# RWKV's core beside the gate tiles: four steps of front per chunk, and both pairs of heads at the same rows

## The reference, cut to what matters

```
S_t = S_{t-1} diag(w_t) + (S_{t-1} a_t) b_t^T + v_t k_t^T ;   y_t = S_t r_t
a = -kk,  b = kk * a_gate,  kk = k*k_k / max(sqrt(sum(kk*kk)), 1e-12)
```

## Time and profile before

| | us |
|---|---|
| median of 3 runs | 2084.71 (2082.78 to 2092.68) |
| the profiled execution | 2090.74 |
| its span | 2089.0 |
| TensorE busy in it | 2033.5 (97%) |
| VectorE, ScalarE, GpSimd busy | 983.1, 775.4, 278.3 |
| mean granted clock of TensorE | 0.985 of full speed |
| the chain that ended last, TensorE's share | 88% |

### The profile page before, as it was taken

The page is one execution under the profiler, slowest core; times in us unless marked ns, Lnnn a source line. Parts: engine busy times, 40 slices in busy tenths (PEclk is TensorE's granted clock), DMA queues, the critical chain, the costliest instruction groups (busy, mean ns, idle before and its releaser), DMA issues.

```text
span 2089.0 us, 27641 instructions
## 1 busy us (share of the span) xinstructions
PE 2033.5 (97%) x11572; PEld 1631.0 (78%) x11572; DVE 983.1 (47%) x1549; ACT 775.4 (37%) x1233; POOL 278.3 (13%) x279
## 2 busy tenths in 40 slices
PE   8989999999999999999999999999899999999997
PEld 6767677777788778888778888888688888888886
DVE  6655555444553233336754544445643432333365
ACT  5573222123444332234533333334322343322345
POOL 1001221210221000012200000001310120100123
PEclk9999999899999999999999999999999999999999
DMA  5111111111633332222421212222232233223221
GB/s 187 57 65 61 47 47 47 41 47 52 222 101 104 101 106 95 97 100 92 161 71 61 71 61 81 84 79 70 81 101 95 98 117 115 101 91 101 92 95 56
DMA packets 59972, 185.47 MB, mean 89 GB/s; under 512 B 6551, under 2 KB 11799, under 8 KB 59720
## 3 DMA queue, kind: packets, MB, share of 16 engines
q1 hardware_dynamic: 59848, 183.71, 26.0%
HBM read 173.46 MB, written 10.22 MB: 88 GB/s over the span
## 4 chain that ended last, share of the span: by engine, by line
PE 88%; DVE 4%; ACT 4%; issue 2%; POOL 1%; DMA 1%; SPq 0%; DVEq 0%; POOLq 0%; ACTq 0%
PE P L561 25%; PE P L563 24%; PE P L562 24%; DVE AREN L1705 1%; PE P L849 1%; PE P L885 1%; POOL AREN L2425 1%; PE P L939 1%; DVE AREN L1708 1%; PE P L878 1%; PE P L937 1%; PE P L834 1%; ACT WHI L1133 1%; PE P L1062 1%; PE P L1028 1%
## 5 line engine op out<-in xcount | busy, mean ns | idle before, releaser
L561 PE MATMUL P<-HH,WHI 128*128 128x512 f32 x1528 | 623.0, 408 | 10.7 <-DVE HL L1725 3.8
L563 PE MATMUL P<-HH,WLO 128*128 128x512 f32 x1528 | 602.2, 394 | 0.0
L562 PE MATMUL P<-HL,WHI 128*128 128x512 f32 x1528 | 601.7, 394 | 0.0
L1133 ACT ACTIVATE WHI<-RAW 128x1024 fp32r<-128x1024 f32 x302 | 317.9, 1053 | 438.3 <-PE P L563 437.5
L1712 DVE TENSOR_TENSOR WLO<-RAW,WHI 128x1024 fp32r<-128x1024 f32 x302 | 374.8, 1242 | 144.6 <-ACT WHI L1133 143.1
L561 PEld LDWEIGHTS P<-HH,WHI 128*128 128x128 f32 x1528 | 289.9, 190 | 89.0 <-issue 15.9
L561 PE MATMUL P<-ARR,WHI 128*128 128x512 f32 (+1 forms) x920 | 353.8, 385 | 0.0
L563 PE MATMUL P<-ARR,WLO 128*128 128x512 f32 (+1 forms) x920 | 352.9, 384 | 0.0
L562 PE MATMUL P<-ARR,WHI 128*128 128x512 f32 (+1 forms) x920 | 352.8, 383 | 0.0
L563 PEld LDWEIGHTS P<-HH,WLO 128*128 128x128 f32 x1528 | 290.3, 190 | 63.1
L562 PEld LDWEIGHTS P<-HL,WHI 128*128 128x128 f32 x1528 | 290.7, 190 | 55.5 <-issue 0.2
(11 more groups left out here) (304 smaller groups left out, 1555.6 us busy)
## 6 DMA issues: line engine op xcount, KB each, us to landing
RAW<-in_w_in_dram SPq DMA_DIRECT2D x117, 512.0 KB, 3.2
RAW<-in_w_ff_dram SPq DMA_DIRECT2D x64, 512.0 KB, 3.2
RAW<-in_w_ml_dram SPq DMA_DIRECT2D x64, 512.0 KB, 3.2
RAW<-in_w_out_dram SPq DMA_DIRECT2D x16, 512.0 KB, 3.2
RAW<-in_w_pg_dram SPq DMA_DIRECT2D x16, 512.0 KB, 3.2
AREN<-in_xT_dram SPq DMA_DIRECT2D x16, 256.0 KB, 5.7
s_gates<-AREN SPq DMA_DIRECT2D x16, 256.0 KB, 2.0
RAW<-in_w_ab_dram SPq DMA_DIRECT2D x8, 512.0 KB, 3.4
```

Of the source, the lines that this page charges most:

```text
L561: e.matmul(out, hi, H[0][:, s], start=first, stop=False)
L562: e.matmul(out, hi, H[1][:, s], start=False, stop=False)
L563: return e.matmul(out, lo, H[0][:, s], start=False, stop=last)
L1133: e.activation(WHI[n % NSPL][:, :], RAW[n % NRAW][:, :], ACT.Copy).then_inc(*D.act.sig("whi", n))
```

## The change

```
-    seq = [["f"], ["f"], ["f"]]
+    seq = [["f"], ["f"], ["f"], ["f"]]
     for what, q, lev in core_steps():
-        seq.append(["c"] + (["f"] if q < 3 and (what in "WN" or (what, lev) == ("la", 3)) else []))
+        seq.append(["c"] + (["f"] if q < 3 and (what in "WN" or (what, lev) in (("la", 3), ("lb", 4))) else []))
     n = len(seq)
-    late = [A_GA + 4 + i * 121 // n for i in range(n)]
-    early = list(range(A_RW + 68, A_GA + 2, 2))
-    rest = n - len(early)
     for i, group in enumerate(seq):
-        put_at = early[i] if i < len(early) else late[(i - len(early)) * (n - 2) // rest]
-        put_steps(at, put_at, group, 0)
-    for i, group in enumerate(seq):
-        put_steps(at, late[i], group, 1)
+        for jj in range(2):
+            put_steps(at, A_GA + 4 + i * 121 // n, group, jj)
@@ tensor_program, front(jj)
                 for q in range(4):
+                    yield
                     b = 6 + jj
                     w.wait_ge(F.act.at("sq", q), free.get(b))
                     (the sum of squares, L781)
@@ pool_program, front(jj)
-                    yield
-                    yield
+                    for _ in range(3):
+                        yield
```

## The result

| | before | after |
|---|---|---|
| median of 6 runs each, us | 2084.86 (2082.78 to 2092.68) | 2075.92 (2072.13 to 2077.07) |
| ratio to before, 95% interval | | 0.9943 (0.9926 to 0.9961) |
| profiled execution, its span | 2090.74, 2089.0 | 2077.07, 2075.3 |

The change makes the kernel faster, by 0.6% by the ratio and 9 us by the medians. Ten more runs of the changed kernel in another batch gave 2076.03 (2074.5 to 2079.39) and 0.9949 (0.9931 to 0.9966). I had forecast 2088, "same". The time lies in the range that I gave, but on the other side of the time before, and where the third rival (the clock behaves as now, 2074) had put it.

What follows compares the result with a forecast made beforehand. It took TensorE as the bound, 88% of the chain and hardly idle in the region. Terms -11.2 - 4.4 + 7.3 + 13 = +4.7, taken as +3.5 us, made 2088 us from 2084.7; range 2073 to 2109.

Steps and rivals of the forecast that it cites:

- the third rival: Clock behaves as now: one fall of 8 us per double O, or falls only behind gaps; about 2074 us, chance 0.15.
- The front's wait: TensorE's wait ahead of L781 goes, 11.2 us over 8 fronts, since a step in between gives cover: -11.2 us.
- The new waits: Both pairs at once: +5.5 us at chunk 0, +3 in chunks 1 to 3, -1.2 at M; +7.3 us.
- Fewer switches: 22 fewer dense rows interrupted by small steps, at 0.2 us each: -4.4 us.
- The clock: Double O's each bring a fall, three of 17.9 us and one of 9, 63 us at half clock: +13 us.
- the main term: The clock's falls; named wrong if intervals at half clock add up to under 45 or over 80 us.
- the signs that I had named: Gate's stage near 314 us, its clock near 0.90, four half-clock intervals of 17 to 18 us but for the last.
- my mark of 2: Forecast wrong altogether if merge or later stages change by over 2 us.
- The rival with the clock staying down: Clock low for most of each chunk from chunk 0's G on: 2109 us, chance 0.25.
- VectorE as the bound: In the gate's stage both pairs' VectorE operations come together, waits +20 us instead of +7.3: 2100 us, chance 0.10.

Runs made afterwards that it cites:

- each half of the change alone: Against the kernel before: only the four steps of front, ratio 0.9921; or only both pairs at the same rows, front in three steps, ratio 0.9999.
- chunk 0's front early: Changed kernel with chunk 0's four lone front steps moved ahead into RWKV's own rows, 180 to 208: 2076.03 us, ratio 0.9936.
- the kernel with four steps of front alone: Four steps of front, but pair 0 keeps its early rows and the rest as before: 2070.06 us, ratio 0.9921 against the kernel before.
- pair 1 a group behind: Changed kernel with pair 1 one group behind pair 0, so no two O steps stand together: 2076.84 us, ratio 0.9950 to the kernel before.
- first row with O in halves: Four steps of front with the rows of before, and each O step cut into two steps of 16 matmuls: 2068.75 us, ratio 0.9917.
- the two kernels with quarters: Changed kernel with each O in four parts, 2064.17 us; the same plus chunk 0's front early and front's second step at lb level 3, 2054.23 us.

## Why the prediction was wrong

**The front's wait** (forecast -11.2): right. L777 waits twice, 1.6 us, both in chunk 0, where the forecast had them.

**The new waits** (+5.5, +3): right in kind, a little high. Chunk 0 costs 1.6 at L777 and 2.7 at G, 4.3 in all; the later chunks 2.3. The place was off: not la's third level behind VectorE but the fourth of lb behind ScalarE's operations. The larger miss is on the other side of the account: the kernel before had 5.5 us of other waits in the region, and I credited only the 1.2 at M and put the other 4.3 at nothing, without a reason. All went, so waits are -11.4 together and not the -3.9 of my terms. In each half of the change alone the waits other than that for the square come to 3 us, so pair 0's place in RWKV's rows alone doesn't explain them.

**Fewer switches** (-4.4 at 0.2 us for each of 22 rows): right in kind, low in size: -7.4, which is 0.34 us a row if all of it is switches. That is no price for an interruption in general: cutting O in quarters interrupts twelve rows more and costs 1.8 us, 0.15 each, less than the 0.23 that I had read at the edges. What makes up the difference no run here takes apart.

**The clock** (+13): the step that failed, with the waits that I left at nothing. Half of it held. Every double O brought a fall, in both traces of the changed kernel, 4.5 to 6.1 us into it in the first, while a single O brings one only sometimes. But the length did not hold. "The clock came back only behind stretches of two dense rows; G (L834) did not raise it" was read from a place where one pair's O stands alone, and made 17.9 us of each fall and 63 in all. Measured are 10.2, 6.8, 10.2 and 10.2 us, and with chunk 0's 3.4 it is 41 (44.4 in the second trace). By the mark that I had set, under 45, the main term is wrong. The place was no fair sample: of the falls at single O's with two dense rows and a G behind them, those at 376.4 and 444.7 did last through G, but the one at 315.0 was back in it, and I had that row and did not weigh it. This is it, in the kernel before:

```profile
314.60 0.51 PE L561 MATMUL P<-HH,WHI 128*128 128x512 f32 x1
314.94 0.59 PE L562 MATMUL P<-HL,WHI 128*128 128x512 f32 x1
...
317.17 2.25 PE L834 MATMUL P<-AREN 64*128 64x128 f32 x16
319.35 0.50 PE L561 MATMUL P<-HH,WHI 128*128 128x512 f32 x1
```

G takes 2.18 us from start to start, between its 1.64 at full and 3.02 at half clock. The fall also began in the dense row behind O, where I had written that it never fell outside O. And a double O is not the same place. In the earlier trace rows the clock fell 1.2 us ahead of the first dense row; in the changed kernel it fell 5.6 us ahead of it (277.2 against 282.80), and so had been down for longer when G came. That this is the reason isn't shown: with chunk 0's front early one fell 5.2 us ahead of it (414.8 against 420.0) and still outlasted G. With both pairs at the same rows, two dense rows behind the O's had the clock back within 1.8 us of G's start in 10 of 11 places of five traces; with one row it came back 3.7 to 4.8 us into G or, in one case, 8.9 us behind G's start. What each fall's length hangs on beyond that I did not settle. In the two traces of the region the clock costs 16.5 us after against 12.6 before, +3.9 instead of +13; by the clocks of all runs, over the whole kernel, it is about +8.

In sum, in the region's traces, the clock term was 9 us too high, waits 7.5 and switches 3, which is 20 us. The sum for the region was +4.7 and came out at -15. Outside it the kernel got 3 us longer, which I had at nothing. With the clock at +8 and all else as forecast, my terms would still have given no change; the waits and the switches turned it into a gain. The range held the time since it reached to the case where the clock term is nothing. Of the signs that I had named, the clock over the gate's stage is 0.93 (near 0.90 forecast) and the stage 293 us (near 314). The first merge rows (336 to 399) take 2.5 us more than before in the first pair of traces and 1.1 in the second, the first of these over my mark of 2: TensorE's wait for the weights' low part there is 2.5 us instead of 1.8, and a fall of 3.4 us stands right behind it.

The time is that of the third rival, but its mechanism is only half of what happened, and that the time fits is luck. It had the clock cost what it cost before (measured +3.9 in the region, about +8 in all), and waits and switches that were too high by as much made up for that. It had one fall of 8 us at each double O, or falls only behind gaps; there was one at each, of 6.8 to 10.2 us, and without a gap. The Trainium skill ("TensorE: Matmul & The Clock Gate", section "Why this matters for your kernels") ties falls to idle gaps. Here some falls do stand beside gaps: the one at 222.6 stands behind waits of 0.8 and 1.9 us and went when those were taken away, and in the kernel with four steps of front alone one at 256.1 stands at a wait of 2.2 us. But the four large ones begin where TensorE has been busy without a gap, and cutting that run into pieces removed them with the waits left standing (8.2 us against 6.9).

The rival with the clock staying down is refuted: no fall outlasts 10.2 us in the two traces of the changed kernel. VectorE as the bound too: TensorE's waits for it are 0.8 us in the region.

**What stays open.** In one of the eleven places (chunk 0's front early, in the interval that holds 420.0) the clock stayed down through G in spite of two rows ahead. At some single O's a fall comes in one execution and not in the next, and a run of 4.1 us brought one at all four places when a single row and the other pair's O followed. What sets that, and how long a fall lasts, is open.

## What to carry to other kernels

When steps of a serial recurrence ride between dense work, count the unbroken run of small matmuls that a new order makes: two runs of 4 us put together cost clock each time (20 of 20 places), and the same work in pieces of 2 us did not. Give a stage whose operand is made by two other engines a step of its own ahead of its use before joining streams. As long as the clock moves by itself, taking out a wait of 2 to 4 us may not show; settle the clock first and then take the waits. And read the clock of every run, not only of the traced one: it told here what single traces did not.

## What the runs showed of the hardware

- TensorE's clock fell with the engine 100% busy: at each of the 20 places with a run of O's 64-wide 32-bit matmuls of 8.2 us at full clock, in five traces; at 8 of 16 with a run of 4.1 us in the two traces of the kernel before (in it or up to 0.4 us behind it); at none of the 32 with a run of 2.06 us in the two kernels with quarters.
- It stayed at half for 23.9 us with the engine busy for all of them, in two kernels (pair 1 a group behind, from 344.1; first row with O in halves, from 298.5).
- Behind a double O, two dense rows at half clock (2.86 us) had it back within 1.8 us of G's start in 10 of 11 places; one row did in none.
- The time at half clock differs between executions of one kernel, from 37 to 71 us in 24 runs of the kernel before, and each us of it goes with about 0.4 us of time.
- 22 fewer interruptions of the dense rows by small steps went with 7.4 us, 0.34 each; twelve more, by quarters of O, with 1.8 us, 0.15 each.
